# Two units of weights ahead of each of five norms: products of x times scale, with the token factor and a bias applied as they leave PSUM

## The reference

```python
def rmsnorm(x, w):
    r = lax.rsqrt(jnp.mean(x32 * x32, axis=-1, keepdims=True) + EPS)
    return (x32 * r).astype(x.dtype) * w
def modulate(h, shift, scale):
    return h * (1 + scale) + shift
# trunk_layer, once for each of 2 layers
xl = xl + 0.5 * g1l * swiglu(modulate(rmsnorm(xl, norm_w[0]), sh1l, sc1l), w_ffn1_in, w_ffn1_out)   # norm1
hl = modulate(rmsnorm(xl, norm_w[1]), sh2l, sc2l)                                                    # norm2
mix_l, mix_c = token_mixer(hl, hc, w_in, ...)
xl = xl + g2l * mix_l
xl = xl + 0.5 * g3l * swiglu(modulate(rmsnorm(xl, norm_w[2]), sh3l, sc3l), w_ffn2_in, w_ffn2_out)   # norm3
```

## Time and profile before

| | |
|---|---|
| median of 3 runs | 2497.06 us (2493.27 to 2498.05) |
| the profiled execution | 2492.84 us, span 2491.0 us |
| PE busy | 2345.1 us, 94% of the span |
| DVE, ACT, POOL busy | 1146.9, 829.7, 171.3 us |
| granted TensorE clock, mean | 0.956 |

### The profile page before, as it was taken

The page is one execution under the profiler, slowest core; times in us unless marked ns, Lnnn a source line. Parts: engine busy times, 40 slices in busy tenths (PEclk is TensorE's granted clock), DMA queues, the critical chain, the costliest instruction groups (busy, mean ns, idle before and its releaser), DMA issues.

```text
span 2491.0 us, 31535 instructions
## 1 busy us (share of the span) xinstructions
PE 2345.1 (94%) x12784; PEld 1886.1 (76%) x12784; DVE 1146.9 (46%) x1970; ACT 829.7 (33%) x1305; POOL 171.3 (7%) x114
## 2 busy tenths in 40 slices
PE   5999999999999999999999999999997996889998
PEld 3777777775777777777777787689996885658888
DVE  2233222437643222233332224775544767457984
ACT  3222222324342222223222224354444454332233
POOL 1000001014000000000000010310011003000001
PEclk7999999999999999999999998999998997789999
DMA  6444444220124444434444422324552221013433
GB/s 262 172 177 178 176 176 191 84 98 17 52 106 178 181 176 170 177 146 152 179 178 176 159 104 100 119 85 170 187 194 90 90 103 49 1 39 144 154 139 136
DMA packets 48310, 340.13 MB, mean 137 GB/s; under 512 B 5168, under 2 KB 7216, under 8 KB 7344
## 3 DMA queue, kind: packets, MB, share of 16 engines
q1 hardware_dynamic: 47136, 337.15, 36.2%
q10 hardware_dynamic: 1040, 1.05, 0.1%
HBM read 337.13 MB, written 1.05 MB: 136 GB/s over the span
## 4 chain that ended last, share of the span: by engine, by line
PE 88%; DVE 6%; ACT 2%; issue 1%; DMA 1%; POOL 1%; SPq 0%; ACTq 0%; DVEq 0%; POOLq 0%
PE bank L451 44%; PE bank L459 22%; PE bank L852 6%; PE bank L425 4%; PE bank L480 3%; PE bank L693 1%; DMA raw<-stream 1%; PE bank L672 1%; PE bank L503 1%; PE bank L652 1%; DVE h L1619 1%; PE bank L681 1%; PE bank L649 1%; ACT w_hi L900 1%; PE bank L509 1%
## 5 line engine op out<-in xcount | busy, mean ns | idle before, releaser
L1273 DVE TENSOR_TENSOR w_lo<-raw,w_hi 128x1024 fp32r<-128x1024 f32 (+1 forms) x389 | 469.1, 1206 | 1082.6 <-ACT w_hi L900 1082.0
L900 ACT ACTIVATE w_hi<-raw 128x1024 fp32r<-128x1024 f32 (+1 forms) x389 | 403.4, 1037 | 1176.2 <-PE bank L451 1155.8
L451 PE MATMUL bank<-h_hi,w_hi 128*128 128x512 f32 (+1 forms) x2024 | 704.2, 360 | 2.7 <-DVE h_lo L1495 1.4
L451 PE MATMUL bank<-h_lo,w_hi 128*128 128x512 f32 (+1 forms) x2024 | 695.3, 356 | 0.0
L451 PEld LDWEIGHTS bank<-h_hi,w_hi 128*128 128x128 f32 x2024 | 383.6, 190 | 82.8 <-issue 28.0
L459 PE MATMUL bank<-h_hi,w_lo 128*128 128x512 f32 (+1 forms) x2024 | 430.3, 355 | 5.1 <-DVE w_lo L1273 5.1
L451 PEld LDWEIGHTS bank<-h_lo,w_hi 128*128 128x128 f32 x2024 | 383.9, 190 | 52.7 <-issue 0.5
L459 PEld LDWEIGHTS bank<-h_hi,w_lo 128*128 128x128 f32 x2024 | 341.7, 190 | 58.9 <-DVE w_lo L1273 6.0
L451 PE MATMUL bank<-hidden_hi,w_hi 128*128 128x512 f32 (+1 forms) x880 | 296.4, 351 | 2.5 <-ACT w_hi L900 2.5
L451 PE MATMUL bank<-hidden_lo,w_hi 128*128 128x512 f32 (+1 forms) x880 | 293.4, 348 | 0.0
L451 PEld LDWEIGHTS bank<-hidden_hi,w_hi 128*128 128x128 f32 x880 | 167.2, 190 | 33.5 <-issue 13.2
(11 more groups left out here) (217 smaller groups left out, 1945.4 us busy)
## 6 DMA issues: line engine op xcount, KB each, us to landing
raw<-stream SPq DMA_DIRECT2D x317, 1024.0 KB, 4.8
x<-x_in SPq DMA_DIRECT2D x1, 2048.0 KB, 9.9
consts<-consts_in SPq DMA_DIRECT2D x1, 1136.5 KB, 5.5
x<-ctx_in ACTq DMA_DIRECT2D x1, 1024.0 KB, 6.7
out<-x SPq DMA_DIRECT2D x2, 512.0 KB, 3.0
params<-params_in SPq DMA_DIRECT2D x1, 413.5 KB, 3.0
```

The lines of the kernel that those rows point to most:

```text
L451: last = nc.tensor.matmul(acc, w_hi[:, buffer, kc, :], v(first_chunk + kc), start=start and kc == n == 0, stop=False)
L900: nc.scalar.activation(w_hi[:, buffer, 0:chunks, :], raw[at % RING][:, 0:chunks, sub * P:(sub + 1) * P], ACT.Copy)\
L1273: nc.vector.tensor_tensor(w_lo[:, buffer, 0:chunks, :], raw[at % RING][:, 0:chunks, sub * P:(sub + 1) * P], w_hi[:, buffer, 0:chunks, :].b ...
```

## The change

For norm20, norm30, norm11, norm21 and norm31 (`DELAYED`), the first two units of the next product no longer wait for the norm. While the stage before is still running, ACT makes the rounded x·scale of each chunk (`raw_high`) and DVE the rest (`raw_low`), in a second operand area. PE multiplies the two units with these (`delayed_unit`). In each of their four halves it also multiplies w_hi and w_lo with the shift in two parts (`shift_parts`, four columns), which gives the bias W'·shift. The sum of squares and the spreading of the token factor stand inside the first half: POOL now adds all 8 squares, so 4 sums remain, and the factor is spread with 4 matmuls in place of the diagonal blocks. DVE multiplies the two units' results with the factor `norm_scale` and adds the bias (in the up-projection ACT adds the gate's bias inside Silu). Meanwhile DVE and POOL scale x in turn (`scaled`, 3 buffers), and the true h_hi and h_lo are made as before; the third unit waits for all 8 chunks of them.

In the diff below the first `delayed_norm` is ACT's and the second DVE's; its `then_first` moves the first unit's bias (`move_bias`) and multiplies its results with the factor.

```diff
+            def delayed_unit(name, unit, accs, start, marks):
+                for sub in range(2):
+                    pe.wait_ge(half_high, At.half + 1)
+                    for kc in range(KC):
+                        if unit == sub == 0 and kc in (0, KC - 2, KC - 1):
+                            pe.wait_ge(sem("raw_ready"), raw_parts(name, max(kc + 1, KC - 2)))
+                        for k, v in enumerate((hi, lo)):
+                            last = nc.tensor.matmul(accs[sub], w_hi[:, buffer, kc, :], v(kc), start=kc == k == 0, stop=False)
+                    if unit == sub == 0:
+                        pe.wait_ge(sem("square_added"), adds_before(name) + adds(name))
+                        for tc in range((T - t0) // P):
+                            last = nc.tensor.matmul(bank[SUM_BANK][:, tc:tc + 1], square_sum[:, t0 + tc * P:t0 + (tc + 1) * P],
+                                                    ones[:, 0:1], start=tc == 0, stop=True, skip_group_check=True)
+                    pe.wait_ge(half_ready, At.half + 1)
+                    if At.biases:
+                        pe.wait_ge(sem("bias_moved"), At.biases)
+                    for kc in range(KC):
+                        nc.tensor.matmul(bias, w_hi[:, buffer, kc, :], shift_parts[:, kc, :], ...)
+                        nc.tensor.matmul(bias, w_lo[:, buffer, kc, :], shift_parts[:, kc, :], ...)
+                        last = nc.tensor.matmul(accs[sub], w_lo[:, buffer, kc, :], hi(kc), start=False, stop=kc == KC - 1)
+                    if unit == sub == 0:
+                        pe.wait_ge(sem("rinv_ready"), DELAYED.index(name) + 1)
+                        for tc in range((T - t0) // P):
+                            last = nc.tensor.matmul(bank[SUM_BANK][:, tc * P:(tc + 1) * P], norm_rinv[:, tc:tc + 1].broadcast_to([P, P]),
+                                                    ident, start=True, stop=True, skip_group_check=True)
...
+            def raw_high(name, kc):
+                act.wait_ge(x_updated, KC * (UPDATED[name] - 1) + kc + 1)
+                for which, a, b in halves(name):
+                    nc.scalar.activation(areas[RAW_AREA[name]][0](kc)[:, a:b], x[:, kc, a:b], ACT.Copy, scale=scales[:, kc, which:which + 1])
...
+            def delayed_norm(name, first, second, after_bias):
+                for kc in range(ADDED, KC):
+                    raw_high(name, kc)
+                    square(name, kc)
+                nc.scalar.activation(small[:, 72:73], const("eps"), ACT.Sqrt)
+                convert(first, 1)
+                act.wait_ge(sem("norm_summed"), n + 1)
+                nc.scalar.activation(norm_rms[:, 0:(T - t0) // P], bank[SUM_BANK][:, 0:(T - t0) // P], ACT.Sqrt, ...)
+                convert(second, 0)
+                act.wait_ge(sem("rinv_spread"), n + 1)
+                nc.scalar.activation(norm_scale[:, t0:], bank[SUM_BANK][:, 0:T - t0], ACT.Copy).then_inc(sem("scale_moved"), 1)
+                for kc in range(KC + 1):
+                    modulate(name, kc)
+                    if kc == 3:
+                        convert(second, 1)
...
+            def raw_low(name, kc):
+                for k, (which, a, b) in enumerate(halves(name)):
+                    dve.wait_ge(sem("raw_high"), raw_parts(name, kc) + k + 1)
+                    nc.vector.scalar_tensor_tensor(lo, x[:, kc, a:b], scales[:, kc, which:which + 1], hi.bitcast(F32), ALU.mult, ALU.subtract)
...
+            def delayed_norm(name, first, second, then_first, then):
+                convert(first, 1)
+                dve.wait_ge(sem("rms_ready"), n + 1)
+                nc.vector.reciprocal(...).then_inc(sem("rinv_ready"), 1)
+                convert(second, 0)
+                dve.wait_ge(sem("scale_moved"), k + 1)
+                for kc in range(KC + 2):
+                    if kc < KC and kc % 2 == 0:
+                        if kc >= N_SCALED:
+                            dve.wait_ge(sem("h_ready"), before + kc - N_SCALED + 1)
+                        nc.vector.tensor_tensor(scaled[:, kc % N_SCALED, t0:], x[:, kc, t0:], norm_scale[:, t0:], ALU.mult)
+                    if 1 <= kc <= KC:
+                        nc.vector.tensor_scalar(target, target, s, b, ALU.mult, ALU.add).then_inc(sem("h_lat_ready"), 1)
+                    if kc >= 2:
+                        nc.vector.tensor_tensor(lo(c)[:, t0:], scaled[:, c % N_SCALED, t0:], hi(c)[:, t0:].bitcast(F32), ALU.subtract)
+                    if kc == 4:
+                        then_first()
+                        convert(second, 1)
+                        then()
```

More of the change, by code:

```diff
@@ L51 @@
 PAIRS = 3
+N_SCALED = 3
 MH = 4
@@ L245, in diags_before @@
         def diags_before(name):
-            return sum((T - t0) // P for _, _, t0 in NORMS[:NORM_AT[name]])
+            return sum((T - t0) // P for other, _, t0 in NORMS[:NORM_AT[name]] if other not in DELAYED)
         def before_updates(update):
@@ L411, in _ @@
             class At:
-                half, turned = 0, 0
+                half, turned, norms, biases, spreads = 0, 0, 0, 0, 0
             def side_sum(at):
@@ new lines, in modulate @@
+            def modulate(name, kc):
+                hi = areas[OPERAND_AREA[name]][0]
+                t0 = START[name]
+                if t0 == 0 and kc < KC:
+                    act.wait_ge(sem(f"h_scaled{kc % 2}"), h_scaled(name, kc))
+                    s, b = modulation(name, kc, 1)
+                    own.mark(nc.scalar.activation(scaled[:, kc % N_SCALED, 0:CTX], scaled[:, kc % N_SCALED, 0:CTX], ACT.Identity, bias=b, scale=s))
+                if kc > 0:
+                    act.wait_ge(sem("h_lat_ready"), h_before(name) + kc)
+                    own.wait(own.n - (1 if kc < KC and t0 == 0 else 0))
+                    nc.scalar.activation(hi(kc - 1)[:, t0:], scaled[:, (kc - 1) % N_SCALED, t0:], ACT.Copy).then_inc(sem("h_high"), 1)
@@ L967, in swiglu, with down @@
                 last = (UP - 1, (UP - 1) % PAIRS)
-                down(name, norm_after, lambda: silu(*last), lambda: high(*last))
-            def down(name, norm_after, *ahead):
+                down(name, norm_after, lambda: silu(*last), lambda: high(*last), then=THEN.get(norm_after))
+            def down(name, norm_after, *ahead, then=None):
                 for n in range(2 * 4 * len(GROUPS)):
@@ new lines, in delayed_product @@
+                def delayed_product(p=0):
+                    dve.wait_ge(sem("bias_moved"), RAW_UNITS * DELAYED.index(norm_name) + p + 1)
+                    dve.wait_ge(sem("silu_ready"), UP * f + p + 1)
+                    for which, a, b in halves(norm_name):
+                        last = nc.vector.scalar_tensor_tensor(squares[:, p, a:b], squares[:, 3, a:b], delayed_bias[p][1][which],
+                                                              squares[:, p, a:b], ALU.add, ALU.mult)
+                        own.mark(last) if which else None
+                    own.wait(own.n)
+                    last.then_inc(sem("pair_moved"), 1)
```

309 lines of the change are left out of this document (245 added, 64 removed).

## The result

The changed kernel takes **2503.64 us** (median, 2499.41 to 2514.41), the kernel before 2493.17 in the same series: a ratio of 1.0049, 95% interval 1.0034 to 1.0064, so it is 10.5 us slower. The forecast was 2504.0. The time is right, but two small errors cancel in it: I added the change to a median of three, 2497.06, which further runs brought down by 3.9 us, and the change itself I put at +7.4 instead of +10.5. That the two cancel is luck.

The account below looks back on a forecast made before the run. The prediction took PE to bound the kernel, with the chain of waits on it for 88% of the span. At full clock -6.6 us, plus 14 for the clock, gave +7.4 on the median 2497.06: 2504 us, range 2486 to 2522.

Parts of the forecast that it names:

- The price of the bias matmuls: First two units of each delayed norm: 64 new small matmuls at 0.113 us, 7.2 us of PE time per norm.
- Rival 2: Bias matmuls cost less than a weight load, 0.063 us each: 2488, or 2474 with a full clock; chance 0.08.
- The stretches at a full clock: PE from the previous stage's last product to the third unit, at five norms: together -6.6 us if the clock holds.
- the 14 us: Clock falls in about four of five norms, 7 us at half speed, 3.5 us lost each: +14 us.
- rival B: Run 1's forecast: idle gaps, not small matmuls, set the clock; stretches 145 to 150, whole 2483 to 2490 us.
- Rival 1: Clock holds through the five stretches: -6.6 us, 2490, between 2486 and 2494; chance 0.25.
- The true h: Ahead of the third unit: last chunk at 30.7 us, PE wants it at 31.6; cover 0.9 us, costed at nothing.
- Rival 3: True h late before the third unit, POOL's products slower beside DVE: +5, 2510; chance 0.15.
- Rival 4: Clock stays low through the 256-wide units at norm31 and norm21: +28, 2525, half of it 2515; chance 0.15.

Follow-up runs that it names:

- run 2: Changed kernel with each half's 16 bias matmuls in one row ahead of the second pass's eight large ones, not in pairs between them; 2503.11 us.
- run 12: The changed kernel measured again without any edit, on the same chip as three other runs; 2503.68 us, ratio 1.0039 to the kernel before.
- run 8: Changed kernel with each bias matmul streaming its 4 shift columns 32 times over, 128 columns in all, outputs unchanged; 2497.43 us.
- run 3: Changed kernel with each bias matmul streaming 256 columns of the raw operand instead of the shift, so biases are wrong; 2497.08 us.
- Run 1: Changed kernel with only the first of eight pairs of bias matmuls left in each half, so biases are wrong; 2486.64 us.
- run 4: Changed kernel with three more full-width matmuls, results unused, ahead of the wait for the sum of squares; 2502.50 us.
- run 7: Changed kernel with DVE scaling all eight chunks of x and POOL none; 2498.47 us.
- run 6: Changed kernel without the bias matmuls that use w_lo, a small part of the bias; 2493.21 us.

## Why the prediction was right, and where it was off

**The price of the bias matmuls: right.** 0.113 us each from the nearest 128-weight-column rows; 0.113 measured between large ones, 0.111 in a row (run 2). 320 of them are 36 us. Rival 2 is out.

**The stretches at a full clock: 2.4 us too short.** Less half of the low-clock time they are 31.9, 33.7, 34.1, 29.7 and 21.3 us; I had put 31.9, 33.8, 33.8, 29.7 and 21.4. But where the clock did hold they are longer: 32.73 at norm20 (run 12), 33.65 at norm30, 34.35 at norm11 and 22.75 at norm31 (run 8, whose groups take the same time). Norm21 never kept its clock; 29.7 is a lower bound, since halving takes off too much. That is at least 153.2 us, a gain of 4.2 at most and not of 6.6.

Halving the low time had hidden two things. A low clock covers waits: 0.7 us ahead of the third unit at norm20, and 0.89 for `bias_moved` at norm31 (run 8). And at norm31 a step of 256 columns takes 0.21 us at the low clock (1686.49 to 1686.70) and 0.12 at the full one (1679.06 to 1679.18), less than twice. Against my terms, norm20 has 1.3 us of waits (1.1 put) and 31.4 of work (30.8 put), norm31 2.06 of waits (1.8 put) and 20.5 of work (19.65 put), so the sum was short in both. At norm21 the waits that I had put at 4.0 came out at 3.8 beside a low clock. The waits that no low clock touched: 0.62 us for the sum at norm20 (0.8 put), and 1.45 and 0.84 at norm21 (0.95 and 1.6 put). POOL's addition was quicker than the row that I used, the last raw chunk later; the two cancel.

**The clock: it fell as forecast, and the 14 us are about right, in part by luck.** "It falls in about four of five norms", at 6 to 7 us, and stays for 7 us: four of five in one execution, three of five in the other (and all five in run 2's), for 6.83 us. Half of the low-clock time is 17.1 and 13.7 us. Against 153.2 us at a full clock the first execution lost 167.75 - 153.2 = 14.5 us at most. In it two things that I had not put are about equal: norm21 falls twice, the second time behind its 1.5 us wait for `bias_moved`, which I had counted as a wait and not as a place for a fall; and elsewhere a fall costs 2.0 to 3.2 us instead of 3.4, for the two reasons above. So the stretches came to +10.4 in place of +7.4: at least 2.4 us from the full-clock sum, at most 0.5 from the clock. The medians differ by as much, but one execution can't show that they do so for the same reasons.

**What the clock did before.** The prediction names a low clock at norm30 and norm21 only. By the earlier trace rows it was low at all five, for about 50 us in all, against 34 in the changed kernel. Less of it lay under PE's work: at norm30 PE was busy for 6.22 of 10.24 us. Filling the gaps has not made the clock low for longer; it has put PE's work where the clock is low.

**What it falls behind.** I named the small matmuls; the rule of the Trainium skill ("TensorE: Matmul & The Clock Gate", "Why this matters for your kernels") names idle gaps. Runs 3 and 8 speak for the first: the same number of matmuls with more columns gave back 9.4 and 10.0 us of the low-clock part. Run 1 shows that my account was one-sided: it came out in rival B's range, and the clock fell just behind waits of 3.64, 3.55 and 2.44 us. So the Trainium skill's rule holds here as well, but it is not enough, as run 4 shows at norm20. Rival 1, the clock held, did not happen with small matmuls; even with wider ones (run 8) the kernel came to 2497.4, as norm21 goes on losing. Its 2490 is my sum; with the stretches as measured it would be 2493 at least.

**The true h: cover about right, the step behind it missed.** I put its last chunk 30.7 us after the start; it came at 31.4 (run 12), at 29.8 with POOL idle (run 7). Rival 3's mechanism, DVE and POOL in each other's way, is real and costs 1.7 us in the stretches' steady sum, not 5; the median gave back 5.2, most of it in the low-clock part, for a reason that is open. What ends PE's wait at norm20 is ACT's conversion behind two squares, a step that I had not listed. It cost 0.7 us at most in the changed kernel, and 3.64 and 2.23 as soon as bias matmuls went (runs 1 and 6).

**Rival 4** did not come: the clock was back after 6.83 us at norm31, all of whose units are narrow.

## What to carry to other kernels

With 128 weight columns a matmul of 4, 32 or 128 moving columns took 0.11 us here, so count small ones by their number, and if a stretch is full of them, look at the granted clock there: up to 128 columns were free, and more columns gave part of the clock back. A low clock costs only where PE sets the pace: beside a busy DVE, 7 us of it more or less changed nothing (0.50 against 0.62 over 30.04 us). And half of the low time is more than it costs where it covers waits. Before work is taken off the bounding engine, list what it covers on every other engine, order of issue included: two thirds of 18 us were gained here, one third went into waits, the largest of them for a conversion that stood behind other work. Where the clock's pattern changes from one execution to the next, compare medians of many, and use one profile only for places and causes.

## What was not expected of the hardware

The granted clock of the same code differed between executions: 6.83 us at the low level at norm20 in one, none in the other. DVE's operation on two SBUF operands took 1.78 us while POOL's ran and 0.68 beside nothing, and POOL's 1.85. And with POOL's scaling gone, the low-clock part of the whole, 92 to 94 us in the changed kernel, was 85.5; the cause is open. The whole gain is clear of noise (2498.5 against twice 2503.7), but that it lies in the clock rests on means with standard errors of 1.6 to 3 us.
